# The values of the paired attentions in passes over two query blocks, and the second maximum of a double step taken in the first

## The reference

```
def chunked_rel_attention(q, k, v, rel_bias):      # 8 heads of 64; "causal" below
    scores = einsum('bcqhd,bckhd->bhcqk', qc, kb) * (HEAD_DIM ** -0.5) + bias
    scores = where(valid, scores, NEG_INF)
    probs = softmax(scores, axis=-1)
    out = einsum('bhcqk,bckhd->bcqhd', probs, vb)

def windowed_gqa(u, w_in, sink, w_out):            # 16 heads of 64; "banded" below
    logits = einsum('bqkgd,bskd->bkgqs', q_blk, k_blk) * scale - slopes * dist
    logits = where(valid, logits, NEG_BIG)         # a window of 128 to either side
    probs = softmax(concatenate([logits, sink_col]))[..., :-1]
    out = einsum('bkgqs,bskd->bqkgd', probs, v_blk)
    return (out * silu(z)) @ w_out
```

## Time and profile before

| | us |
|---|---|
| median of 3 runs (1635.49 to 1638.23) | 1635.6 |
| the profiled execution | 1634.16 |
| its span in the trace | 1632.4 |
| from the first scores of the causal attention to its last values | 197.7 to 369.0 |
| from the first scores of the banded attention to its last values | 980.2 to 1120.5 |

### The profile page before, as it was taken

The page is one execution under the profiler, slowest core; times in us unless marked ns, Lnnn a source line. Parts: engine busy times, 40 slices in busy tenths (PEclk is TensorE's granted clock), DMA queues, the critical chain, the costliest instruction groups (busy, mean ns, idle before and its releaser), DMA issues.

```text
span 1632.4 us, 20230 instructions
## 1 busy us (share of the span) xinstructions
PE 1495.0 (92%) x7122; PEld 1185.4 (73%) x7122; DVE 982.9 (60%) x1549; ACT 737.9 (45%) x1265; POOL 236.8 (15%) x218
## 2 busy tenths in 40 slices
PE   5898798989987999999998999998998989999897
PEld 3686576767765888887885787887776768778775
DVE  5669876455765555554224547885463467788454
ACT  4424454652334545544123326664442446656342
POOL 3006622221110000000000000111110011222111
PEclk9999899988998999999999999999999999999999
DMA  9532133325621232232321322112222120000321
GB/s 386 193 98 90 52 110 109 116 78 176 219 70 48 81 103 93 87 103 90 101 92 52 110 77 59 59 46 78 90 78 91 52 79 25 27 27 17 113 78 64
DMA packets 39883, 151.68 MB, mean 93 GB/s; under 512 B 4784, under 2 KB 4928, under 8 KB 39040
## 3 DMA queue, kind: packets, MB, share of 16 engines
q1 hardware_dynamic: 29664, 105.92, 20.3%
q0 software_dynamic: 10144, 44.76, 7.6%
HBM read 144.37 MB, written 6.29 MB: 92 GB/s over the span
## 4 chain that ended last, share of the span: by engine, by line
PE 74%; DVE 13%; ACT 6%; issue 5%; DMA 1%; POOL 0%; DVEq 0%; ACTq 0%; SPq 0%; POOLq 0%
PE ps L604 22%; PE ps L605 22%; PE ps L606 22%; PE ps L727 3%; ACT w_hi L1024 2%; DVE w_lo L1477 2%; PE ps L696 2%; PE ps L661 2%; DVE c_acc L1554 1%; DMA w_raw<-in_w 1%; PE ps L681 1%; DVE tmp L1679 1%; DVE a_lo L1684 1%; DVE acc_b L1525 0%; DVE pt_lo L1614 0%
## 5 line engine op out<-in xcount | busy, mean ns | idle before, releaser
L604 PE MATMUL ps<-a_hi,w_hi 128*128 128x512 f32 x880 | 360.5, 410 | 19.8 <-ACTq L1301 11.8
L605 PE MATMUL ps<-a_lo,w_hi 128*128 128x512 f32 x880 | 350.4, 398 | 0.0
L606 PE MATMUL ps<-a_hi,w_lo 128*128 128x512 f32 x880 | 350.3, 398 | 0.0
L1477 DVE TENSOR_TENSOR w_lo<-w_raw,w_hi 128x1024 fp32r<-128x1024 f32 x130 | 166.3, 1281 | 165.6 <-ACT w_hi L1024 164.9
L604 PEld LDWEIGHTS ps<-a_hi,w_hi 128*128 128x128 f32 x880 | 167.2, 190 | 64.9 <-ACTq L1301 12.7
L606 PEld LDWEIGHTS ps<-a_hi,w_lo 128*128 128x128 f32 x880 | 166.9, 190 | 40.9
L605 PEld LDWEIGHTS ps<-a_lo,w_hi 128*128 128x128 f32 x880 | 167.5, 190 | 36.1 <-issue 0.5
L1024 ACT ACTIVATE w_hi<-w_raw 128x1024 fp32r<-128x1024 f32 x138 | 144.5, 1048 | 72.9 <-PE ps L606 56.6
L604 PE MATMUL ps<-b_hi,w_hi 128*128 128x512 f32 x240 | 99.6, 415 | 10.5 <-DVE b_lo L1849 5.5
L605 PE MATMUL ps<-b_lo,w_hi 128*128 128x512 f32 x240 | 96.8, 403 | 0.0
L606 PE MATMUL ps<-b_hi,w_lo 128*128 128x512 f32 x240 | 96.6, 402 | 0.0
(11 more groups left out here) (306 smaller groups left out, 3132.7 us busy)
## 6 DMA issues: line engine op xcount, KB each, us to landing
w_raw<-in_w SPq DMA_DIRECT2D x198, 512.0 KB, 3.5
ada_a<-in_ada POOLq DMA_DIRECT2D x16, 512.0 KB, 8.0
ada_g<-in_ada POOLq DMA_DIRECT2D x16, 512.0 KB, 3.8
ada_b<-in_ada POOLq DMA_DIRECT2D x16, 512.0 KB, 4.2
x_resid<-in_x POOLq DMA_DIRECT2D x2, 2048.0 KB, 11.8
pl_store<-pl_out POOLq DMA_DIRECT2D x2, 2048.0 KB, 9.0
pl<-pl_store POOLq DMA_DIRECT2D x2, 2048.0 KB, 9.7
alibi<-in_alibi POOLq DMA_DIRECT2D x16, 192.0 KB, 2.7
```

The lines of the kernel that those rows point to most:

```text
L604: pe.matmul(o, w[0], r[0], start=start, stop=False, skip_group_check=skip)
L605: pe.matmul(o, w[0], r[1], start=False, stop=False, skip_group_check=skip)
L606: return pe.matmul(o, w[1], r[0], start=False, stop=stop, skip_group_check=skip)
L1477: dve.tensor_tensor(w_lo[:, n % SLOTS, :], w_raw[:, n % RAW, :], w_hi[:, n % SLOTS, :].bitcast(F32), ALU.subtract).then_inc(w_lo_done, 1)
```

## The change

It has three parts, for the causal and the banded attention only.

**Values.** `pt` is laid out by key block: the four steps of two query blocks (t = 0 and 1, or 2 and 3) and two heads share it, with the columns of query blocks t and t+1 of one head side by side. A new list, `over_keys`, says for either half of the query blocks which key blocks are taken with which columns, and `half_values` goes through it, for one head and two query blocks at a time, with passes of 256 columns where both query blocks see the key block and of 128 where one does. It stands in the turns i for which step i-5 has an odd t (i mod 8 = 3, 4, 7, 0), and ahead of the transposes of that turn. The instructions that write `pt` keep their number and their sizes, but write in pieces of 128 columns with a step of 512 between them, and ScalarE waits for the values of the half before it (`v_half` for the first head, `lin_done` for the second).

**Maxima.** In VectorE's even turns the maximum of step i+1 is taken behind the low part of step i-3, ahead of `after`. Odd turns have none.

**Wiring.** The list of the third attention moves from a variable of its own into the object; nothing of its work changes.

```
         class Attn:
+            def turned(self, i):
+
+                _, t = self.step(i)
+                b, e = self.spans[t]
+                at = 2 * P * (i % 2) + P * (t % 2)
+                return [pt[:, b:e, at:at + P] for pt in self.pt], slice(P * b, P * e)
...
-                     p1, (pt1_hi, pt1_lo), causal, lambda j: tile1["o", j])
+                     p1, (pt1_hi, pt1_lo), causal, lambda j: tile1["o", j], [[(0, 0, 2), (1, 1, 2)], [(0, 0, 2), (1, 0, 2), (2, 0, 2), (3, 1, 2)]])
...
-                     p2, (pt2_hi, pt2_lo), band, lambda j: o2_at[j])
+                     p2, (pt2_hi, pt2_lo), band, lambda j: o2_at[j], [[(0, 0, 2), (1, 0, 2), (2, 1, 2)], [(2, 0, 2), (3, 0, 2), (1, 0, 1)]])
...
-            def pair_values(a, i):
-
-                pe.wait_ge(pt_ready, a.n0 + i + 2)
-                h, t = a.step(i)
-                b, e = a.spans[t]
-                tile = a.lin(h + t // 2)
-                if t % 2 == 0:
+            def half_values(a, i):
+
+                pe.wait_ge(pt_ready, a.n0 + i + 1)
+                (h, t), j = a.step(i), i % 2
+                tile = a.lin(h // 2 * 2 + t // 2)
+                if j == 0:
                     free_bank(tile)
-                for j in range(2):
-                    at, slot = 2 * P * j + t % 2 * P, (a.n0 + i + j) % 4
-                    for s in range(b, e):
-                        m = mm3(ps[:, tile % LIN, at:at + P], a.v(h + j, s), tuple(pt[:, slot, P * s:P * s + P] for pt in a.pt),
-                                s == b, s == e - 1, skip=True)
-                m.then_inc(lin_done if t % 2 else v_half, 1)
+                o = ps[:, tile % LIN, 2 * P * j:2 * P * j + 2 * P]
+                keys = a.over_keys[t // 2]
+                for c, (s, t0, t1) in enumerate(keys):
+                    r = tuple(pt[:, s, 2 * P * j + P * t0:2 * P * j + P * t1] for pt in a.pt)
+                    m = mm3(o[:, P * t0:P * t1], a.v(h, s), r, c == 0, c == len(keys) - 1, skip=True)
+                m.then_inc(lin_done if j else v_half, 1)
...
                     if between is not None:
                         between(i)
+                    if 0 <= i - 5 < a.steps and a.step(i - 5)[1] % 2:
+                        half_values(a, i - 5)
                     if 0 <= i - 3 < a.steps:
                         turn(a, i - 3)
-                    if i % 2 == 0 and 0 <= i - 6 < a.steps:
-                        pair_values(a, i - 6)
                     after(i)
...
             def pair_turn_hi(a, i):
-                if t % 2 == 0 and (t or pair):
-                    act.wait_ge(v_half, a.n0 // NT + 2 * pair + t // 2)
-                elif t == 3 or pair:
-                    act.wait_ge(lin_done, a.lin(2 * pair + t // 2 - 1) + 1)
+                part = 2 * pair + t // 2
+                if part and i % 2 == 0:
+                    act.wait_ge(v_half, a.n0 // NT + part)
+                elif part:
+                    act.wait_ge(lin_done, a.lin(part - 1) + 1)
...
                 for i in range(a.steps + 2 * NT):
-                    if i < a.steps:
+                    if i < a.steps and i % 2 == 0:
                         pair_maxima(a, i)
...
                     if 0 <= i - 1 < a.steps:
                         norms(a, i - 1)
+                    if i < a.steps and i % 2 == 0:
+                        pair_maxima(a, i + 1)
```

More of the change, by code:

```diff
@@ L381, in build, with __init__ @@
         class Attn:
-            def __init__(self, heads, n0, q, k, vv, pbuf, pt, spans, lin):
+            def __init__(self, heads, n0, q, k, vv, pbuf, pt, spans, lin, over_keys):
                 self.heads, self.n0, self.q, self.k, self.v = heads, n0, q, k, vv
-                self.p, self.pt, self.spans, self.lin = pbuf, pt, spans, lin
+                self.p, self.pt, self.spans, self.lin, self.over_keys = pbuf, pt, spans, lin, over_keys
                 self.p_at, self.steps = 1 if pbuf is p2 else 0, NT * heads
@@ L399, in build @@
         n2 = n1 + NT * A_HEADS
-        part_keys = [[(s, 0, 2) for s in range(4)], [(s, 2, 4) for s in range(4)]]
         attn1 = Attn(H1, 0, lambda h: (qk_hi[half(h), h // 2, :], qk_lo[half(h), h // 2, :]),
@@ L411, in build @@
                      lambda h, s: (vb_hi[:, s, P * (h // 2):P * (h // 2) + P], vb_lo[:, s, P * (h // 2):P * (h // 2) + P]),
-                     p3, (pt3_hi, pt3_lo), full, lambda h: tile3["o", h])
+                     p3, (pt3_hi, pt3_lo), full, lambda h: tile3["o", h], [[(s, 0, 2) for s in range(4)], [(s, 2, 4) for s in range(4)]])
         used_at = {}
@@ L758, in values3 @@
                 o = ps[:, attn3.lin(h) % LIN, :]
-                for i, (s, t0, t1) in enumerate(part_keys[part]):
+                for i, (s, t0, t1) in enumerate(attn3.over_keys[part]):
                     if i // 2 == keys_half:
@@ L1097, in pair_turn_hi @@
                 h, t = a.step(i)
-                pair, (b, e) = h // 2, a.spans[t]
+                pair = h // 2
                 act.wait_ge(t_done, n + 1)
-                if t % 2 == 0 and (t or pair):
-                    act.wait_ge(v_half, a.n0 // NT + 2 * pair + t // 2)
-                elif t == 3 or pair:
-                    act.wait_ge(lin_done, a.lin(2 * pair + t // 2 - 1) + 1)
-                act.activation(a.pt[0][:, n % 4, P * b:P * e], ps[:, T_BANK + n % 2, P * b:P * e], ACT.Copy).then_inc(pt_hi_done, 1)
+                part = 2 * pair + t // 2
[3 more added lines that the diff above has]
+                    act.wait_ge(lin_done, a.lin(part - 1) + 1)
+                (hi, _), turned = a.turned(i)
+                act.activation(hi, ps[:, T_BANK + n % 2, turned].rearrange("p (s q) -> p s q", q=P), ACT.Copy).then_inc(pt_hi_done, 1)
             def turn_hi3(h, t):
@@ L1605, in pair_turn_lo @@
                 n = a.n0 + i
-                b, e = a.spans[a.step(i)[1]]
+                (hi, lo_), turned = a.turned(i)
                 dve.wait_ge(pt_hi_done, n + 1)
-                dve.tensor_tensor(a.pt[1][:, n % 4, P * b:P * e], ps[:, T_BANK + n % 2, P * b:P * e],
-                                  a.pt[0][:, n % 4, P * b:P * e].bitcast(F32), ALU.subtract).then_inc(pt_ready, 1)
+                dve.tensor_tensor(lo_, ps[:, T_BANK + n % 2, turned].rearrange("p (s q) -> p s q", q=P), hi.bitcast(F32),
+                                  ALU.subtract).then_inc(pt_ready, 1)
             def turn_lo3(i):
```

## The result

The changed kernel takes 1618.32 us (median of 4 runs, 1616.47 to 1618.82), the kernel before 1635.55 (4 runs on the same chip, 1634.9 to 1638.23): 17.2 us less, a ratio of 0.989 with a 95% interval of 0.9872 to 0.9907. Forecast were 1599 us and a move of 36.6. The time lies just above the upper end of the range, 1618.

The account below looks back on a forecast made before the run. TensorE was taken as the limit, working throughout in the banded attention and waiting for maxima in the causal. Banded 16.4 plus causal 20.2 made 36.6 us off 1634.16, giving 1597.6; runs' median 1.4 higher, so 1599 (1588 to 1618).

Parts of the forecast that it names:

- The passes: Both attentions: 60 passes of 128 columns a pair become 36, 24 of them 256 wide; a pair falls by 2.49 us.
- Rival D: Both attentions: a pass's pace follows its columns, so joining gives nothing and only waits go; 17 us, 1619; chance 0.02.
- F: Whole kernel: no effect to be measured, because the gains lie off the path; chance 0.04.
- B: VectorE takes over as limit; banded pair 16.7 us, banded gain 8.8, causal 10.7, together 19.5, so 1616; chance 0.26.
- the last 24.4 us, credited with 2.3: Banded attention's end, without gate blocks, hanging on VectorE and ScalarE: 2.3 us gain (1 to 2.5) from fewer passes.
- the loop of 3.75 us a double step: Banded attention: scores, values, transposes, high part, low part, second maximum, next scores; 3.75 us, just fitting TensorE's 3.80.
- 7.3 forecast: Causal attention up to 281.4, where VectorE's loop sets the mean's start: gain 7.3 us (3.9 to 10).
- the term of 3.9: Causal attention up to the mean: eight odd maxima leave VectorE's loop, 0.49 us each in the mean, 3.9 together.
- that of 3.4: Causal attention up to the mean: part of TensorE's 8.2 us of waits, returning to VectorE as late transposes, goes; 3.4 (0 to 6).
- 10.3 forecast: Causal attention, 281.4 to 348.5: the 5.3 us wait, slow-clock work and passes go; sum 11.3, taken as 10.3 (5 to 11.3).
- 2.6 forecast: Causal attention's end, 348.5 to 369: fewer passes, but last probabilities only some 1.2 us earlier; gain 2.6 us (0 to 5).
- E: Slower by the clock: the loop outgrows TensorE's work, passes run at 1.2 GHz, banded pair 18.8 us; 1644; chance 0.04.

Follow-up runs that it names:

- four together: Changed kernel with adds held, second maximum ahead of the low part, convolution's mean one step later, VectorE's second gating part moved to step 31: 1593.7 us, ratio 0.9742.
- five together: The kernel of four together, with one GpSimd add near the causal attention's end held until the last low part is taken: 1590.0 us, ratio 0.9724.

## Where the prediction was right and where it failed

By the profiled executions the spans are 16.1 us apart, against 36.6 in the sum; the two attentions account for 15.5. The passes and the banded pairs came as forecast. What failed is the step from earlier maxima to an earlier mean: where GpSimd's adds would then fall was put at nothing (7.3 us forecast there, 0.8 came). The ends of both attentions failed too (2.6 and 2.3 forecast, -3.5 and -1.8 came), because less work of TensorE met waits that stayed, with a slow clock behind them, and so did the mean (3.0).

**The passes were right.** 288 of 256 columns and 144 of 128 stand where I had them; of the banded attention:

```profile
L610 PE MATMUL ps<-pt_hi,va_hi x96: 222/282/580, 986.4 to 1104.6; 128*128 128x256 f32 x64, 128*128 128x128 f32 x32
```

That is one pass of three, so 192 and 96, and half as many in the causal attention. Six passes of 256 take 0.71 us from start to start, 0.118 each:

```profile
1041.43 0.28 PE L610 MATMUL ps<-pt_hi,va_hi 128*128 128x256 f32 x1
...
1042.14 0.23 PE L610 MATMUL ps<-pt_hi,va_hi 128*128 128x128 f32 x1
```

Rival D is out, and so is F.

**The banded attention: 16.4 forecast, 10.9 came.** The first pair gave 1.2 (forecast 1.5) and the 5.75 pairs 11.5 (12.6): 15.7 us a pair for 15.5, far from the 16.7 of B, and the reason given for the margin, the normalising under GpSimd's subtraction, was the right one (15.2 without it). VectorE's waits for high parts fell as said, from 17.3 to 9.9 us in that stretch. The step of this sum that failed is **the last 24.4 us, credited with 2.3**. They went to 26.2, a loss of 1.8. There are no gate blocks in there, so TensorE has less work than the loop of 3.75 us a double step that I had worked out a few lines above, and it stands 1.35, 1.10 and 1.14 us for maxima; its double steps take 3.61 and 3.70 us, the 3.75 of that loop. I held the loop against TensorE's 3.80 us with gate blocks and not against its work without them. So these four double steps take 14.89 us after 14.80, with fewer passes in them. Behind that the clock is 0.77 where it was 1.00 before, and the rest takes 11.3 us after 9.6. That second part may be chance: behind the same waits the clock stayed at 1.00 in the profiled execution with the mean later.

**The causal attention up to the mean: 7.3 forecast, 0.8 came.** This is the largest miss. I had said that if VectorE's loop were not shorter by some 7 us, the term of 3.9 or that of 3.4 would be wrong. The loop, maximum of step 0 to that of step 16, took 77.0 us after 77.8. The two terms had come in part: without the adds it is 70.3 before and 66.2 after, 4.1 less of the 7.3. The other 3.2 are open. The larger thing missing was a term: where GpSimd's adds fall. I had read the collision in the banded attention, written that the place "can shift", and given it no price and no rival. The rows for it were there before the change: VectorE's two taps took 3.46 and 3.55 us beside an add instead of 1.4, and each add started behind the exponential of an odd step, the step whose maximum was to be moved.

**281.4 to 348.5: 10.3 forecast, 7.3 came** from the start of the mean to the scores of step 30. From step 18 on it is 63.6 to 53.3, the 10.3 to the tenth. That exact meeting is luck in part: with the adds left out the same stretch goes from 66.1 to 52.0. The other 3.0 are the mean itself, 3.60 to 6.61 us at a clock of 0.54. I had announced the wait for the last taps ("under 2 us") but not charged what TensorE does slowly behind it, though the earlier trace rows had the price.

**The end: 2.6 forecast, -3.5 came** (20.5 to 24.0 us). TensorE comes 7.4 us sooner to the scores of step 30, and VectorE and ScalarE do not: their splits, gate's parts and products in front of the last two normalisings keep their place, one of the normalisings collides (2.0 us; with the adds held the end still takes 21.3), and TensorE, having stood 6.3 us, makes the last passes slowly.

**The rivals.** The sum of B (1616) is closest to the result, but its mechanism, a banded attention bound by VectorE at 16.7 us a pair, did not come. So the time fell near B for reasons that no rival held. E, the clock, was wrong as a price for the whole, but right in kind: the slow stretch behind the new wait took 3.0 us in the mean, and others took part of both ends.

The Trainium skill ("SBUF — State Buffer", section "Who interferes with whom") names which instructions of VectorE share ports with GpSimd: those with two inputs in SBUF, and a multiplication by a column in a fast mode; one with a single SBUF input outside such a mode is free. The runs agree in each case: normalisings (2.15 for 0.40 us), taps and subtractions within SBUF (2.83 for 0.68) are held, maxima and low parts that read PSUM are not. With that rule and the 14 adds of the trace before, the new neighbours of each could have been written down ahead of the run; that this would have given the right time is not shown.

What stays open: the 13 us or so between the change's worth without adds (23) and the forecast are located by the profile (the ends of both attentions, the mean, and some 3 us of VectorE's loop); the slow end of the causal attention was moved about (four and five together) but not shortened. What a shorter chain on ScalarE would give there wasn't tried.

## What to carry to other kernels

When an instruction is moved to another place on an engine, write down what the engines that follow it will do at their new times, and what stands under them there: an add on GpSimd that was harmless beside a maximum out of PSUM cost 1.5 to 2.4 us each time it met a normalising or a tap in SBUF. A wait that holds such an add until the partner reads PSUM cost nothing that could be seen and gave 17 us here, as much as the change itself. And where TensorE's work is cut, ask at each stretch what comes second: the saved passes were worth 11.5 us where TensorE was the limit, and nothing where it then stood, and went on slowly.

## What the runs showed of the hardware

The collision works both ways; in the two cases that show it, what had begun first kept its time. A subtraction in SBUF that had begun 0.26 us ahead of GpSimd's add kept its 0.69 us, and the add took 2.63 instead of 2.38. With four together the add started while a gate's part in SBUF was running and took 2.85 (the gate's part kept its 1.29), and the subtraction behind that part waited for the add in turn, 2.83 instead of 0.68.

TensorE's granted clock after a wait was steeper than I had priced: the same eight passes with the ones matrix took 3.60 us with work ahead of them, 5.30 behind a wait of 3.0 us, and 6.61 behind one of 4.8. It doesn't go with the length of the wait alone: with the maxima alone they took 5.29 behind 4.1 us. The stretch of 6.61 reads 0.54, close to the lower of the two levels (1.2 GHz of 2.4). And the same work behind the same waits, at the end of the banded attention, took 9.56 us at 1.00 in one execution and 11.28 at 0.77 in another.
